# A decoder layer on one core: six places for centring the convolution rows, and the mean subtracted again in the output phase

## The reference

```python
z = jnp.einsum("bsd,de->bse", h, w_in) + b_in
glu_val, glu_gate, gate_c, q, k, v, f_logit, gate_a = _split_columns(z)
# _conformer_conv: u = glu_val * sigmoid(glu_gate); c = depthwise conv of u, plus b_dw
#   c = _layer_norm(c, g_cn, b_cn); return silu(c)
y_conv = _conformer_conv(glu_val, glu_gate, w_dw, b_dw, g_conv_norm, b_conv_norm)
y_conv = y_conv * jax.nn.silu(gate_c)
y_attn = _forgetting_attention(q, k, v, f_logit) * jax.nn.silu(gate_a)
sub = jnp.einsum("bse,ed->bsd", jnp.concatenate([y_conv, y_attn], axis=-1), w_out) + b_out
h = _layer_norm(DN_ALPHA * h + sub, g_post, b_post)
```

## Time and profile before

| | us |
|---|---|
| median of three runs | 1600.45 |
| lowest and highest of them | 1598.1, 1602.7 |
| the profiled execution | 1602.69 |
| its span (first to last event of the core) | 1600.9 |

### The profile page before, as it was taken

The page is one execution under the profiler, slowest core; times in us unless marked ns, Lnnn a source line. Parts: engine busy times, 40 slices in busy tenths (PEclk is TensorE's granted clock), DMA queues, the critical chain, the costliest instruction groups (busy, mean ns, idle before and its releaser), DMA issues.

```text
span 1600.9 us, 29447 instructions
## 1 busy us (share of the span) xinstructions
PE 1557.6 (97%) x11574; PEld 1491.3 (93%) x11574; DVE 1443.0 (90%) x1952; ACT 839.4 (52%) x1224; POOL 274.8 (17%) x295
## 2 busy tenths in 40 slices
PE   7999999999999999999999999999998899999997
PEld 6989999999999999999999999999888888888885
DVE  7669999999999999999999999999967689996787
ACT  5565454554545545455454454554454476744462
POOL 1101112122021121211212212121223200000000
PEclk9999999999999999999999999999999999999998
DMA  8488888999989999899998999998998989887875
GB/s 225 112 199 188 225 203 211 237 210 241 234 204 234 210 249 227 206 238 233 230 221 213 238 232 225 223 222 218 209 276 236 269 296 347 301 232 248 258 213 182
DMA packets 316761, 367.33 MB, mean 229 GB/s; under 512 B 14593, under 2 KB 254369, under 8 KB 315313
## 3 DMA queue, kind: packets, MB, share of 16 engines
q1 hardware_dynamic: 284880, 260.45, 53.1%
q0 software_dynamic: 27360, 100.68, 34.5%
q10 hardware_dynamic: 4384, 4.33, 0.8%
HBM read 286.73 MB, written 87.06 MB: 233 GB/s over the span
## 4 chain that ended last, share of the span: by engine, by line
PE 79%; DVE 9%; DMA 5%; issue 4%; ACT 1%; SPq 1%; POOL 0%; DVEq 0%; ACTq 0%; POOLq 0%
PE ps L1056 26%; PE ps L1057 26%; PE ps L1058 26%; DMA cin<-conv_rows_dram 3%; DVE whl L1308 3%; DVE c_tiles L1409 2%; PE ps L1173 1%; DMA raw<-raw 1%; DVE raw L1327 1%; DMA f_raw<-in_w_in_dram 1%; DMA conv_rows_dram<-c_tiles 1%; DVE raw L1319 1%; SPq L402 1%; DVE xl L1347 0%; ACT whl L781 0%
## 5 line engine op out<-in xcount | busy, mean ns | idle before, releaser
L1056 PE MATMUL ps<-xh,whl 128*128 128x256 f32 x3136 | 897.4, 286 | 22.2 <-DVE whl L1308 10.4
L1057 PE MATMUL ps<-xl,whl 128*128 128x256 f32 x3136 | 889.2, 284 | 0.0
L1058 PE MATMUL ps<-xh,whl 128*128 128x256 f32 x3136 | 889.1, 284 | 0.0
L781 ACT ACTIVATE whl<-raw 128x1024 fp32r<-128x1024 f32 x392 | 415.2, 1062 | 552.7 <-PE ps L1058 441.8
L1056 PEld LDWEIGHTS ps<-xh,whl 128*128 128x128 f32 x3136 | 601.2, 192 | 27.2 <-issue 13.8
L1057 PEld LDWEIGHTS ps<-xl,whl 128*128 128x128 f32 x3136 | 601.6, 192 | 0.5 <-issue 0.5
L1058 PEld LDWEIGHTS ps<-xh,whl 128*128 128x128 f32 x3136 | 601.3, 192 | 0.0
L1308 DVE TENSOR_TENSOR whl<-raw,whl 128x1024 fp32r<-128x1024 f32 x392 | 482.5, 1231 | 61.4 <-ACT whl L781 61.3
L1409 DVE SCALAR_TENSOR_TENSOR c_tiles<-ps,taps,c_tiles 128x511 f32<-128x511 f32 (+14 forms) x480 | 350.6, 730 | 6.8
L630 POOL DMA_DIRECT2D raw<-raw x56 | 49.9, 891 | 483.4 <-DMA raw<-in_w_in_dram 427.3
L1311 DVE TENSOR_TENSOR whl<-raw,whl 128x1024 fp32r<-128x1024 f32 x80 | 97.8, 1223 | 32.4 <-ACT whl L757 32.2
(11 more groups left out here) (185 smaller groups left out, 1552.6 us busy)
## 6 DMA issues: line engine op xcount, KB each, us to landing
raw<-in_w_in_dram SPq DMA_DIRECT2D x224, 512.0 KB, 8.1
raw<-raw POOLq DMA_DIRECT2D x112, 512.0 KB, 6.1
out_sums_dram<-in_w_out_dram POOLq DMA_DIRECT2D x64, 512.0 KB, 9.7
raw<-out_sums_dram SPq DMA_DIRECT2D x64, 512.0 KB, 5.1
raw<-in_w_out_dram SPq DMA_DIRECT2D x48, 512.0 KB, 5.2
out_sums_dram<-in_w_out_dram SPq DMA_DIRECT2D x32, 512.0 KB, 9.4
out_sums_dram<-out_sums_dram SPq DMA_DIRECT2D x32, 512.0 KB, 9.6
x<-in_x_dram SPq DMA_DIRECT2D x8, 512.0 KB, 8.1
```

Of the source, the lines that this page charges most:

```text
L781: nc.scalar.activation(w_high(n), source(n), ACT.Copy).then_inc(high_done, 1)
L1056: nc.tensor.matmul(o, ah, bh, start=start, stop=False, skip_group_check=True)
L1057: nc.tensor.matmul(o, ah, bl, start=False, stop=False, skip_group_check=True)
L1058: return nc.tensor.matmul(o, al, bh, start=False, stop=True, skip_group_check=True)
```

## The change

- `cin` gets six places, of which two are `rstd` and a tile that held the mean; the mean itself goes to `csum`. A load of tile j now waits for the square of tile j - 6, not for a square and a store of tile j - 4. The places of the loads in SP's order stay.
- ACT no longer stores the centred tiles; each square moves one slot later. The output phase loads the uncentred rows, and `norm` subtracts the mean before it multiplies: 16 more operations of 128 x 512 on DVE, each with a wait for the one before.
- Four loads of attention and convolution rows ahead of the output phase (`load_a`, `load_c`) move later in SP's order.
- At the end, token tile 0 goes the way of tiles 2 and 3: DVE scales it, ACT multiplies, POOL adds `b_post` by DMA, half after half, and SP stores. Its two statistics are taken behind each product, the inverse stands between its two scalings. Tile 1 is scaled, finished and stored in quarters, the inverse laid between the scalings.
- Some semaphores are merged into one, with no other order.

```diff
+CIN = 6
...
-        mean = sb("mean", [P, SEQ], F32, over)
+        cin_5 = sb("cin_5", [P, SEQ], F32, over)
...
+        mean = csum
...
-        var_row, root_tmp = c_tiles[:, 0, :], csum[:, :]
+        var_row, root_tmp = c_tiles[:, 0, :], c_tiles[:, 1, :]
...
+        def cin_slot(j):
+            n = j % CIN
+            return cin[:, n, :] if n < 4 else (rstd, cin_5)[n - 4][:, :]
...
-                if j >= 4:
-                    sp.wait_ge(sq_done, j - 3)
-                    sp.wait_ge(cent_stored[j % 4], 16 * (j // 4))
-                sp.dma_start(cin[:, j % 4, :], conv_dram[j, :, :]).then_inc(cin_loaded[j % 4], 16)
+                if j >= CIN:
+                    sp.wait_ge(sq_done, j - CIN + 1)
+                sp.dma_start(cin_slot(j), conv_dram[j, :, :]).then_inc(cin_loaded[j % CIN], 16)
...
             load_a(0, 0)
-            load_a(0, 1)
             sp.wait_ge(low_done, at(g, 2) + 1)
             sp.wait_ge(t4_in[g % 2], parity(g))
             load_out(3)
-            sp.wait_ge(unit_done, at(g, 2) + 1)
-            load_a(0, 2)
-            for n in range(4):
-                sp.wait_ge(cent_stored[n], 64)
-            sp.wait_ge(unit_done, at(g, 3) + 1)
-            load_c(0)
+            load_a(0, 1)
             sp.wait_ge(low_done, at(g, 4) + 1)
             load_out(4)
-            load_a(0, 3)
+            load_c(0)
...
+                if u in (6, 10):
+                    load_a(0, 2 if u == 6 else 3)
...
-            for t in (2, 3):
+            for e, t in enumerate((2, 3, 0)):
                 for h in range(2):
                     c = slice(1024 * h, 1024 * (h + 1))
-                    sp.wait_ge(bpost_added, 16 * (2 * (t - 2) + h + 1))
+                    sp.wait_ge(bpost_added, 16 * (2 * e + h + 1))
                     sp.dma_start(out[0, P * t:P * (t + 1), c], res[t][:, c]).then_inc(stored, 16)
-            for t in range(2):
-                for h in range(2):
-                    c = slice(1024 * h, 1024 * (h + 1))
-                    sp.wait_ge(row_done, 2 * t + h + 1)
-                    sp.dma_start(out[0, P * t:P * (t + 1), c], res[t][:, c]).then_inc(stored, 16)
-            sp.wait_ge(stored, 32 * NT)
+            for n in range(4):
+                c = slice(SEQ * n, SEQ * (n + 1))
+                sp.wait_ge(row_done, n + 1)
+                sp.dma_start(out[0, P:2 * P, c], res[1][:, c]).then_inc(stored, 16)
+            sp.wait_ge(stored, 160)
...
-            for t in (2, 3):
+            for e, t in enumerate((2, 3, 0)):
                 for h in range(2):
                     c = slice(1024 * h, 1024 * (h + 1))
-                    if (t, h) != (2, 0):
-                        pool.wait_ge(bpost_added, 16 * (2 * (t - 2) + h))
-                    pool.wait_ge(rows_scaled, 2 * (t - 2) + h + 1)
+                    if e + h:
+                        pool.wait_ge(bpost_added, 16 * (2 * e + h))
+                    pool.wait_ge(rows_scaled, 2 * e + h + 1)
                     repeat_row(res[t][:, c], b_post[c], bpost_added, True)
...
-                nc.scalar.dma_start(conv_dram[j, :, :], cin[:, j % 4, :]).then_inc(cent_stored[j % 4], 16)
-                nc.scalar.activation(c_tiles[:, j % 2, :], cin[:, j % 4, :], ACT.Square).then_inc(sq_done, 1)
+                nc.scalar.activation(c_tiles[:, j % 2, :], cin_slot(j), ACT.Square).then_inc(sq_done, 1)
...
-                    if HEAD_GROUPS + 3 <= g < HEAD_GROUPS + 7 and s in (2, 4, 5):
-                        square(4 * (g - HEAD_GROUPS - 3) + (2, 4, 5).index(s))
-                    if HEAD_GROUPS + 3 < g <= HEAD_GROUPS + 7 and s == 0:
+                    if HEAD_GROUPS + 3 <= g < HEAD_GROUPS + 7 and s in (3, 5, 6):
+                        square(4 * (g - HEAD_GROUPS - 3) + (3, 5, 6).index(s))
+                    if HEAD_GROUPS + 3 < g <= HEAD_GROUPS + 7 and s == 1:
                         square(4 * (g - HEAD_GROUPS - 4) + 3)
...
-            def scale_rows(t):
-                act.wait_ge(fin_vec, INVERSE_AT[t - 2] + 4)
+            def scale_rows(e):
+                act.wait_ge(fin_vec, INVERSE_AT[e] + 4)
                 for h in range(2):
-                    act.wait_ge(scaled_done, 2 * (t - 2) + h + 1)
-                    r = res[t][:, 1024 * h:1024 * (h + 1)]
-                    nc.scalar.activation(r, r, ACT.Copy, scale=rs[:, t - 2:t - 1]).then_inc(rows_scaled, 1)
+                    act.wait_ge(scaled_done, 2 * e + h + 1)
+                    r = res[(2, 3, 0)[e]][:, 1024 * h:1024 * (h + 1)]
+                    nc.scalar.activation(r, r, ACT.Copy, scale=rs[:, e:e + 1]).then_inc(rows_scaled, 1)
...
             deviation(2)
+            scale_rows(2)
             deviation(3)
...
-                dve.wait_ge(cin_loaded[j // 4], 80)
+                dve.wait_ge(cin_loaded[j // 4], 64)
                 dve.wait_ge(rstd_vec, 5)
                 o = yc_tile(j)
+                vec.tensor_tensor(o, o, mean[:, :], ALU.subtract).then_inc(norm_done, 1)
+                dve.wait_ge(norm_done, 2 * j + 1)
                 vec.tensor_tensor(o, o, rstd[:, :], ALU.mult).then_inc(norm_done, 1)
...
-            for e in (2, 3):
-                t = e - 2
-                for g in range(2):
-                    dve.wait_ge(end_done, 2 * t + g + 1)
-                    add_product(2, t, g, t, 0, ALU.add)
-                dve.wait_ge(c11_read, 2 * t + 2)
-                row_stats(t, 0)
-                dve.wait_ge(stats_done, 12 + 2 * t + 2)
-                moments(e)
-                for h in range(2):
-                    scale_half(e, h)
-                inverse(e)
-                dve.wait_ge(fin_vec, INVERSE_AT[e] + 4)
-                dve.wait_ge(scaled_done, 2 * e + 2)
-                for h in range(2):
-                    c = slice(1024 * h, 1024 * (h + 1))
-                    vec.scalar_tensor_tensor(out=res[t][:, c], in0=res[t][:, c], scalar=rs[:, e:e + 1], in1=bpost_b[:, c],
-                                             op0=ALU.mult, op1=ALU.add).then_inc(row_done, 1)
+            def last_product(t, g):
+                dve.wait_ge(end_done, 2 * t + g + 1)
+                add_product(2, t, g, t, 0, ALU.add)
+                dve.wait_ge(c11_read, 2 * t + g + 1)
+                vec.bn_stats(stats[:, t, g, :], result(t, 0, g)).then_inc(stats_done, 1)
+            def scale_quarter(e, n):
+                t, c = (2, 3, 0, 1)[e], slice(SEQ * n, SEQ * (n + 1))
+                vec.scalar_tensor_tensor(out=res[t][:, c], in0=res[t][:, c], scalar=mv[:, 2 * e:2 * e + 1], in1=gpost_b[:, c],
+                                         op0=ALU.subtract, op1=ALU.mult).then_inc(scaled_done, 1)
+            last_product(0, 0)
+            last_product(0, 1)
+            dve.wait_ge(stats_done, 14)
+            moments(2)
+            scale_half(2, 0)
+            inverse(2)
+            scale_half(2, 1)
+            last_product(1, 0)
+            last_product(1, 1)
+            dve.wait_ge(stats_done, 16)
+            moments(3)
+            c, base = slice(3, 4), INVERSE_AT[3]
+            scale_quarter(3, 0)
+            scale_quarter(3, 1)
+            dve.wait_ge(fin_act, 4)
+            vec.reciprocal(rs[:, c], std[:, c]).then_inc(fin_vec, 1)
+            scale_quarter(3, 2)
+            dve.wait_ge(fin_vec, base + 1)
+            vec.scalar_tensor_tensor(out=newton[:, c], in0=rs[:, c], scalar=var_eps[:, c], in1=rs[:, c],
+                                     op0=ALU.mult, op1=ALU.mult).then_inc(fin_vec, 1)
+            scale_quarter(3, 3)
+            dve.wait_ge(fin_vec, base + 2)
+            vec.tensor_scalar(newton[:, c], newton[:, c], -0.5, 1.5, ALU.mult, ALU.add).then_inc(fin_vec, 1)
+            dve.wait_ge(fin_vec, base + 3)
+            vec.tensor_tensor(rs[:, c], rs[:, c], newton[:, c], ALU.mult).then_inc(fin_vec, 1)
+            dve.wait_ge(fin_vec, base + 4)
+            dve.wait_ge(scaled_done, 10)
+            for n in range(4):
+                c = slice(SEQ * n, SEQ * (n + 1))
+                vec.scalar_tensor_tensor(out=res[1][:, c], in0=res[1][:, c], scalar=rs[:, 3:4], in1=bpost_b[:, c],
+                                         op0=ALU.mult, op1=ALU.add).then_inc(row_done, 1)
```

More of the change, by code:

```diff
@@ L352, in build @@
         t_added = [sem(f"t{n + 1}_added") for n in range(4)]
-        cent_stored = [sem(f"cent_stored{n}") for n in range(4)]
         cum_stored, bias_loaded = sem("cum_stored"), sem("bias_loaded")
@@ L356, in build @@
         z1_stored, z2_stored = [sem(f"z1_stored{p}") for p in range(2)], [sem(f"z2_stored{p}") for p in range(2)]
-        cin_loaded = [sem(f"cin_loaded{n}") for n in range(4)]
+        cin_loaded = [sem(f"cin_loaded{n}") for n in range(CIN)]
         a_loaded, z_loaded = [sem(f"a_loaded{n}") for n in range(4)], [sem(f"z_loaded{n}") for n in range(4)]
@@ L975, in y_high @@
                 if v < 2:
-                    for n in range(4):
-                        act.wait_ge(cent_stored[n], 64)
+                    act.wait_ge(sq_done, HEADS)
                 elif v != E0 // 2:
```

46 lines of the change are left out of this document (22 added, 24 removed).

## The result

The changed kernel takes 1607.5 us (median of 6 runs, 1605.0 to 1610.5), the kernel before beside it 1601.6 (6 runs, 1596.5 to 1604.8). The ratio is 1.0042, 95% interval 1.0026 to 1.0059: 6.7 us more (the ratio on 1600.5; the two medians lie 5.9 apart), between 4.2 and 9.4. That is outside the range predicted, and of the other sign.

A forecast was written before the change was run, and what follows sets the result against it. TensorE bounds the kernel, its only large loss being 18.6 us in centring, behind the third tile's load. Centring -12, subtractions +5 and end +3 sum to -4 us: 1596.5 us median, range 1589 to 1605.

The forecast's parts named there:

- the loop through it: Centring: VectorE waits for the third tile, so low parts, weight blocks and the next tile come late; 18.6 us lost.
- The six places at nothing: Centring: the six `cin` places by themselves gain nothing, as SyncE reaches these loads no earlier than before.
- Stores gone and the loop broken, -12 in all: Centring: without stores, the tile wait goes from group 53 on; 12 us saved, between 3 and 17.
- Squares one slot later: nothing gained or lost: Centring: `sum_3` is issued 6.8 us behind the group's start, against 7.1 before; no gain or loss.
- The landing of `sum_3`, taken as 7 us: Centring: its DMA takes 7 us where 6.2 are left, losing 0.8 us in each of four groups.
- the rival that I gave 0.12 and 1606 us: Centring: `sum_3` takes over the wait, landing in 8.5 us or more; 3 us saved, +5 to +6; chance 0.12.
- Sixteen subtractions, +5: Output phase: subtractions in `norm` on VectorE, which has 3.2 us left; 5 us lost, bounds 3 and 8.
- The tail, +3: End: tile 1's stores wait behind tile 0's two accumulating DMAs, 5.5 us each; 2.4 us lost, rounded to 3.
- Loads later, semaphores merged, nothing: Before the output phase: later attention and convolution loads, some 15 us left for the nearest, and merged semaphores cost nothing.
- The four cases: Whole kernel: forecast 0.4, tile's load stays long 0.2, costs mostly hidden or centring loses nothing 0.25, `sum_3` takes over 0.12.
- the three classes: Whole kernel: chances of faster 0.42, within 0.3% (4.8 us) of no change 0.40, slower 0.18.
- the first rival: Centring: the tile's load stays long beside GpSimd's DMAs; 6 us saved, 2 us lost in all, 1602.5; chance 0.2.

The follow-up runs named there:

- e5: Kernel before with `sum_3` issued ahead of the fourth square's addition in GpSimd's queue: 1591.6 us, -8.0 against the kernel before.
- e8: Changed kernel with centred rows stored again, no subtraction, the old tail, and `sum_3` ahead of the fourth addition: 1595.2 us, -4.5 against the kernel before.
- e9: Kernel before with `sum_3` ahead of the fourth addition and the last `csum` addition on VectorE: 1592.0 us, -8.3 against the kernel before.
- e11: Changed kernel with centred rows stored, squares in their old steps, old tail, no subtraction: 1602.5 us, +2.1 against the kernel before.
- e6: Changed kernel with ScalarE's squares back in their old steps: 1601.9 us, +1.0 against the kernel before.
- e4: Changed kernel without the 16 subtractions in `norm`: 1605.1 us, +4.3 against the kernel before.
- e1: Kernel before with the new tail alone: 1605.8 us, +4.2 against the kernel before.
- e2: Changed kernel with the tail of the kernel before: 1606.1 us, +3.8 against the kernel before, 2.9 less than the changed kernel.
- e7: Changed kernel with centred rows stored again, no subtraction and the old tail, squares still later: 1605.8 us, +6.1 against the kernel before.
- e3: Changed kernel with `sum_3` issued ahead of the fourth square's addition: 1598.6 us, -2.7 against the kernel before.
- e12: Changed kernel with `sum_3` ahead, the old tail, and the 16 subtractions on GpSimd: 1600.9 us, +0.2 against the kernel before.

## Why the prediction was wrong, by its steps

- **What bounds the centring stage: the first step that failed.** From the chain I took the load of the third tile as the wait, and the loop through it as the 18.6 us. The load is on the chain, but e5 leaves it there and TensorE loses 1.6 us in the window instead of 13.8. `sum_3`, which GpSimd issues behind the fourth square's addition, is the link whose removal gives the stage back. The loop that I described exists (five waits for low parts, 6.6 us before; 4.2 and 5.0 us in e8 and e9), but it was not what had to be broken first. The wait behind `sum_3` was in the rows too: 2.0 us and a clock of 0.61; I treated it as what comes next, not as the cause.
- **"The six places at nothing": right** (e11, +2.1, at the edge of no change), for the reason given.
- **Stores gone and the loop broken, -12 in all: the term that was most off.** In medians the centring part gave -1.6 (below). For the old order of squares the size was near: e6 against e11 gives -9.4. My account expected the weight blocks 2.4 us behind the group's start; in the changed kernel they are issued 4.1 us behind in group 52 (1181.35), 2.6 in group 53 (1205.26) and 4.0 in group 54 (1228.24).
- **"Squares one slot later: nothing gained or lost": the step that cost the sign.** I compared the new issue of `sum_3`, 6.8 us behind the group's start, with the 7.1 of before, an issue that already was late by a stall. The old order without that stall was the proper measure. Moving the squares back gained 5.7 us (e6). And 6.8 was itself too early: the fourth addition takes 2.2 us beside VectorE's operations and not 1.3, and the issue of 1210.47 stands 7.8 us behind the start of group 53 (1218.39 - 1.18 - 14.55 = 1202.7).
- **The landing of `sum_3`, taken as 7 us:** 8.7, 6.4, 7.5 and 8.7. A later issue and landings near 8 are the rival that I gave 0.12 and 1606 us, and that is what ran. It had 3 us saved in the centring stage; the medians have 1.6 (below), the two profiles 7.3 at the start of the output phase.
- **Sixteen subtractions, +5: right by the profiles.** 5.3 us of output phase (changed 315.5, e4 310.2), with the sign of it where forecast, TensorE waiting for VectorE. The medians give 2.4, with an error of some 3.
- **The tail, +3: right,** also in its mechanism. 14.7 to 14.9 for 11.7 or 11.8 us; e1 +4.2, e2 -2.9. The two DMAs landed in 4.9 and 5.8 us, where I had 5.5 for each, so tile 1's stores were issued at 1597.8, as worked out.
- **Loads later, semaphores merged, nothing: right** for the output phase (with them 310.2 to 310.4 in e4, e7, e8 and e11, without them 308.9 to 310.4 in the kernel before, e1, e5 and e9).
- **The sum.** In medians the change is +6.7, of which 5.3 and 3.0 are the output phase and the tail; that leaves -1.6 us for the centring part (within the interval, -4 to +1). By the chain of runs from before over e11 and e6 to the changed kernel it is places +2.1, stores -9.4, squares +5.7, each with an error of 2 to 3 us, where the forecast had -12 for the three together.
- **The chances.** The four cases had 0.97 together, and the three classes 1.00: the first rival's 0.2 went into them as 0.23.

## What to carry to other kernels

When several engines wait in a ring, the longest piece on the chain need not be the one to remove: look for a queue entry that stands behind late work without needing it, and move that first. One addition put behind the DMA issue it delayed gave -8.0 us. Dropping sixteen stores gave -9.4, against 5.3 for the subtractions that this needs, 5.7 for the new order of the squares and 3.0 for the new tail; with two more places, which gained nothing, the whole change came to +6.7. A wait that is gone may uncover the next: with `sum_3` ahead and the stores kept, two of three profiles (e8 and e9, not e5) show the tile's load again. An issue time measured in a stalled group is no yardstick for a new order: work out the old order without the stall too. And an engine at 96% has no room for sixteen small operations, nor has an idle neighbour that slows it by more than it takes off.

## What the runs showed of the hardware

- An addition of 128 x 512 on GpSimd beside back-to-back VectorE work took either 2.20 us, with VectorE's pair of operations at 3.45 for 2.35, or 6.18 us, until VectorE's first pause. Which of the two comes is not set by this code, which is the same in both kernels (2.20 us in the kernel before, 6.18 in e1).
- GpSimd's accumulating DMA of 512 KB (`sum_3`, groups 52 to 55) landed in 4.6 to 5.7 us when issued ahead of the fourth addition in e3, and in 6.4 to 8.7 when issued behind it in the changed kernel, with the same bytes. In e5, issued ahead too but with the stores kept, it took 5.1 to 8.0. So the place in GpSimd's queue alone doesn't set it; what else was in the DMA queues differs, and no run separates that.
- Sixteen subtractions on GpSimd took 30.1 us, 1.9 each, and those on VectorE 0.7; moving them made the output phase 6.9 us longer (e12 322.9, e3 316.0).
